# A router whose weights become the stationary operand, in four 32-column groups, with the partial sums added by a further product

## The reference

```python
def hier_moe(x, w_rg, b_rg, w_re, b_re, w_gate, w_up, w_down):
    """Top-1 expert group, then top-2 experts within it; gated-MLP experts."""
    pg = jax.nn.softmax(jnp.einsum('bld,dg->blg', x, w_rg).astype(jnp.float32) + b_rg, axis=-1)
    pg_top, g_idx = lax.top_k(pg, 1)
    le = (jnp.einsum('bld,de->ble', x, w_re).astype(jnp.float32) + b_re).reshape(B, L, N_EXPERT_GROUPS, EXPERTS_PER_GROUP)
...
    for e in range(N_EXPERTS):
        hid = jax.nn.silu(x @ w_gate[e]) * (x @ w_up[e])
        y = y + gates[..., e:e + 1] * (hid @ w_down[e])
...
x = x + mix @ w_out
x = x + hier_moe(rmsnorm(x, norm2_g), w_rg, b_rg, w_re, b_re, w_gate, w_up, w_down)
```

## Time and profile before

| | |
|---|---|
| median of three executions | 1037.68 us |
| the profiled execution | 1037.42 us, its span 1035.8 us |
| PE busy | 930.3 us, 90% of the span |
| DVE busy | 431.6 us, 42% |
| ACT busy | 161.7 us, 16% |
| POOL busy | 213.8 us, 21% |
| router, MATMUL records of full tiles | 128, 276 ns in the mean |
| expert part, first product | 593.38 us from the start |

### The profile page before, as it was taken

How to read it: one execution, slowest core, us unless ns; L and a number is a source line. 1 busy time by engine, 2 the same in 40 slices (tenths; PEclk the granted TensorE clock), 3 DMA queues, 4 the chain that set the end, 5 groups by cost and what they waited for, 6 DMA issues and landing times.

```text
span 1035.8 us, 16152 instructions
## 1 busy us (share of the span) xinstructions
PE 930.3 (90%) x6215; PEld 799.8 (77%) x6215; DVE 431.6 (42%) x1157; ACT 161.7 (16%) x454; POOL 213.8 (21%) x301
## 2 busy tenths in 40 slices
PE   6997999999999999999984099999999999999910
PEld 3953866959597786959653099999999999999910
DVE  2235363544626354552665332222222222233378
ACT  1122112121312212121220000011001011010013
POOL 1031030120303012030301322222222222222261
PEclk9999999999999999999996599999999999999965
DMA  9970706043000101010074468888888888788766
GB/s 333 291 224 20 214 1 203 2 136 98 36 27 1 62 1 41 1 41 2 1 285 66 130 217 318 314 299 325 303 300 302 316 315 313 293 295 307 255 207 231
DMA packets 91902, 184.50 MB, mean 178 GB/s; under 512 B 12933, under 2 KB 59589, under 8 KB 83666
## 3 DMA queue, kind: packets, MB, share of 16 engines
q1 hardware_dynamic: 72930, 154.86, 42.9%
q0 software_dynamic: 7328, 19.22, 5.6%
q10 hardware_dynamic: 11600, 9.84, 2.8%
HBM read 142.56 MB, written 41.31 MB: 178 GB/s over the span
## 4 chain that ended last, share of the span: by engine, by line
PE 81%; DVE 6%; DMA 2%; issue 2%; ACT 1%; ACTq 0%; POOL 0%; DVEq 0%; POOLq 0%
PE bank L1172 78%; PE bank L1177 1%; DVE win L1150 1%; DVE xbuf L1124 1%; DVE xn L1124 1%; DMA ids_d<-tokid,slots 1%; DMA win<-ids_d 0%; DMA ye_d<-wout 0%; DMA win<-ye_d,yslot 0%; PE bank L1349 0%; PE bank L1278 0%; DVE sig L783 0%; ACT nsb L641 0%; DVE hT L1124 0%; ACTq L717 0%
## 5 line engine op out<-in xcount | busy, mean ns | idle before, releaser
L1172 PE MATMUL bank<-wout,win 128*128 128x150 f32 x2048 | 265.9, 291 | 27.0 <-DVE wout L1071 27.0
L1172 PEld LDWEIGHTS bank<-wout,win 128*128 128x128 f32 x2048 | 264.2, 190 | 27.0 <-issue 27.0
L1172 PE MATMUL bank<-hT,win 128*128 128x128 f32 (+1 forms) x1536 | 180.7, 279 | 0.0
L1172 PEld LDWEIGHTS bank<-hT,win 128*128 128x128 f32 x1536 | 177.9, 192 | 0.2
L1172 PE MATMUL bank<-win 128*128 128x150 f32 x1024 | 133.6, 290 | 0.0
L1172 PE MATMUL bank<-win,hT 128*128 128x260 f32 (+3 forms) x432 | 130.9, 460 | 1.8 <-DMA win<-in_w_in 1.8
L1172 PEld LDWEIGHTS bank<-win 128*128 128x128 f32 x1024 | 132.0, 189 | 0.0
L1172 PE MATMUL bank<-wout,mixT 128*128 128x512 f32 (+1 forms) x288 | 127.0, 594 | 3.5 <-issue 2.3
L1102 DVE TENSOR_TENSOR win<-bank,win 128x150 f32<-128x150 f32 x64 | 20.2, 315 | 242.1 <-ACT win L713 242.1
L1172 PEld LDWEIGHTS bank<-win,hT 128*128 128x128 f32 (+1 forms) x432 | 78.4, 184 | 50.0 <-issue 37.5
L1172 PEld LDWEIGHTS bank<-wout,mixT 128*128 128x128 f32 (+1 forms) x288 | 50.7, 181 | 66.9 <-issue 65.1
(11 more groups left out here) (251 smaller groups left out, 776.3 us busy)
## 6 DMA issues: line engine op xcount, KB each, us to landing
win<-in_w_gate SPq DMA_DIRECT2D x32, 1024.0 KB, 5.0
win<-in_w_up SPq DMA_DIRECT2D x32, 1024.0 KB, 7.1
win<-in_w_down SPq DMA_DIRECT2D x32, 1024.0 KB, 7.1
ye_d<-zeros SPq DMA_DIRECT2D x4, 4352.0 KB, 18.0
ye_d<-wout ACTq DMA_DIRECT2D x64, 150.0 KB, 5.7
win<-in_w_in SPq DMA_DIRECT2D x4, 2048.0 KB, 19.6
xbuf<-in_x_prompt SPq DMA_DIRECT2D x8, 512.0 KB, 4.4
wout<-in_w_out SPq DMA_DIRECT2D x1, 4096.0 KB, 15.4
```

Source lines behind the costliest of these rows:

```text
L1172: return nc.tensor.matmul(out, lhsT, rhs, start=first, stop=last)
```

## The change

The operands change places. The stationary one is now a piece of `wr`, widened with zeros from 20 to 32 columns, the moving one the piece of h2T. The result comes out turned, logits on partitions and rows along the free axis. Piece k goes to partitions 32q to 32q + 31 of bank 7 with q = k mod 4, so that the bank holds four partial sums of two pieces each. DVE copies the bank out once (`partial_logits`, into lgT). A further product (`router_sums`) has lgT stationary and a 0/1 matrix `stk` (128 x 20, four identities one below the other) moving: it adds the four parts and turns them to rows at once, into columns 128 to 147 of bank 7. `logits` reads from there. `stk` and the zeros are made by POOL before the loop; `ioi` now shares the place of lgT.

```diff
-        wr = sb("wr", [P, KD, NR])
+        wr = sb("wr", [P, KD, 32])
+        stk = sb("stk", [P, NR])
+        lgT = sb("lgT", [P, P])
...
+            link(g.memset(wr[:, :, NR:32], 0.0))
+            link(g.memset(stk[:, :], 0.0))
+            for q in range(4):
+                link(g.affine_select(out=stk[:, :], in_=stk[:, :], compare_op=ALU.not_equal, fill=1.0,
+                                     base=-32 * q, pattern=[[-1, NR]], channel_multiplier=1))
...
+            def partial_logits(t):
+                R = ROWS[t]
+                after(dve, "lo_done", t + 1)
+                v.tensor_copy(lgT[:, 0:R], B[7][:, 0:R]).then_inc(S["lgT_ready"], 1)
+
             def logits(t):
                 R = ROWS[t]
-                after(dve, "lo_done", t + 1)
-                v.tensor_tensor(rt[0:R, 0:NR], B[7][0:R, 0:NR], brt[0:R, :], ALU.add).then_inc(S["lo_read"], 1)
+                after(dve, "lg_done", t + 1)
+                v.tensor_tensor(rt[0:R, 0:NR], B[7][0:R, P:P + NR], brt[0:R, :], ALU.add).then_inc(S["lo_read"], 1)
...
                 for k in range(KD):
-                    last = mm(B[7][0:R, 0:NR], h2T[:, k, 0:R], wr[:, k, :], k == 0, k == KD - 1)
+                    q = k % 4
+                    last = mm(B[7][32 * q:32 * q + 32, 0:R], wr[:, k, :], h2T[:, k, 0:R], k < 4, k >= KD - 4)
                 last.then_inc(S["lo_done"], 1)
+
+            def router_sums(t):
+
+                R = ROWS[t]
+                after(pe, "lgT_ready", t + 1)
+                mm(B[7][0:R, P:P + NR], lgT[:, 0:R], stk[:, :]).then_inc(S["lg_done"], 1)
...
+                if 2 <= i:
+                    router_sums(i - 2)
+                if DECP < i < NT:
+                    cols_by(turn_a(i), i, Q0, "q_done", range(1, 2))
...
-                    cols_by(turn_a(i), i, Q0, "q_done", range(1, 4))
+                    cols_by(turn_a(i), i, Q0, "q_done", range(2, 4))
```

More of the change, by code:

```diff
@@ L117, in hymba_step @@
         iof = sb("iof", [P, 64])
-        ioi = sb("ioi", [P, 64], I32)
+        ioi = lgT[:, 0:64].bitcast(I32)
         tokid = sb("tokid", [P, NT], I32)
@@ L208, in hymba_step @@
                  "u_ready", "dlt_ready", "pm_done", "mixb_ready", "out0_done", "out_done", "x1_ready", "rs20",
-                 "xn2_ready", "x1_stored", "h2_stored", "h2T_done", "h2T_ready", "lo_done",
+                 "xn2_ready", "x1_stored", "h2_stored", "h2T_done", "h2T_ready", "lo_done", "lgT_ready", "lg_done",
                  "lo_read", "rexp_in", "rexp", "route_ready", "rank_done", "rank_read", "slot_ready",
@@ L979, in _ @@
                     numerators(LAST)
+                    partial_logits(LAST - 1)
                     head_out(LAST)
@@ L999, in _ @@
                 if 2 <= i:
+                    partial_logits(i - 2)
                     logits(i - 2)
@@ L1386, in _ @@
                     out_of_pool(LAST, i)
+                    router_sums(LAST - 1)
                     head_transposes(LAST)
```

## The result

The changed kernel takes 1031.84 us (median of 4, 1031.37 to 1032.82) against 1038.09 for the kernel before (4, 1037.40 to 1040.21): ratio 0.9938, 95% interval 0.9920 to 0.9955. It is faster, by more than was forecast (1037.3) and past the low end of the range (1032.0).

A forecast was written before the change was run, and what follows sets the result against it. The prediction took PE to bound the kernel from 90 to 511 us. Six full tiles −1.0, tile 1 +0.27, tile 7 +0.29 and tile 8 0.0 sum to −0.4 against 1037.68, giving 1037.3 us; range 1032.0 to 1042.3.

The forecast's parts named there:

- X: PE time of a full tile's sixteen router records in four column groups; 1.21 us chosen between bounds 0.60 and 1.74.
- the lower bound of 0.60: Lower bound for the sixteen router records: all four groups overlap freely, 15 × 0.033 + 0.109 = 0.60 us.
- The other terms of a full tile: On PE beside the router records: passage 0.20 and stk product 0.22 us, against 1.79 for the old router.
- The passage into 32-column mode: On PE ahead of the router: 0.09 us, with 0.12 for the way back; 0.20 taken for the two.
- rival C: In the router every change of group costs a 0.10 us passage: about 1049 us; chance 0.07, shared with an unseen wait.
- Rival B: In the router all four groups overlap, a product's second record too: −5.2 us, 1032.5 us in all; chance 0.18.
- Tile 1: Decode rows: router records and passages stay as they are; the stk product between 128-column neighbours adds 0.27 us.
- Tile 7: Block i == NT: the copy partial_logits enters DVE's chain to head_transposes, +0.29 us; what PE saves isn't seen.
- Tile 8: Last iteration, clock 0.50: router records −1.01 us, copy, hand-over to PE and stk product +1.05; sum ±0.0.
- Hidden work: Full tiles: copy and moved work cost nothing; mix_start moves under 2 us, against 6.5 us of slack at the ranks.
- The cover of the second block of q: Its 8 products now precede the transpose of HM, moving mix_start by about 1.8 us less the router's saving; no cost.

The follow-up runs named there:

- the repetitions: The unedited changed kernel timed twice more against the kernel before: 1033.40 against 1037.29 us, ratio 0.9962, and 1032.99 against 1037.44 us, ratio 0.9965.
- the order of neighbours: The changed kernel with piece k in column group k // 2 instead of k mod 4: 1033.77 us, ratio 0.9965 to the kernel before.

## Why the prediction was wrong

**The step that failed** is the choice of X: "The two records of one product go to the same group with other weights, so the second must wait for the first, 0.109 us; only the step to the next group can overlap". Its first half is right: one group, two groups and four groups all go at 0.11 a record within a group. The second half is wrong. While one group waits for its own record, the other three go on, in both orders of the program that were run, and so the sixteen records take four rounds. X is 0.48, not 1.21, and below even the lower bound of 0.60. The bound rested on 0.033 us as "the pace at which records with 32-column weights can be issued at all". That was the pace within one group for 20 to 32 moving columns. Between groups the starts are 0.007 apart, and a row of records into one group couldn't show that.

**The other terms of a full tile.** With X = 0.48 the prediction's sum gives 0.20 + 0.48 + 0.22 − 1.79 = −0.89 a tile; the measured is −0.80. The passage into 32-column mode was as read (0.09: the last 260-column record starts at 291.57, 0.219 later the router is due at 291.79, and it starts at 291.88). Behind the router 292.45 − (291.88 + 0.48) = 0.09, and the block of q in between takes 294.34 − 292.45 = 1.89 where sixteen at 0.112 are 1.79, another 0.10. So the way back costs 0.19 and the whole passage 0.28, not 0.20, and 0.28 + 0.48 + 0.22 − 1.79 = −0.81 is the −0.80. A change of the group alone costs no such passage, as the four starts 7 ns apart show; rival C falls, and the Trainium skill (TensorEngine Tiling (Array Packing), Key Properties) is borne out: changing the mode drains the array, changing only the tile doesn't.

**Rival B**, −5.2 in all, was the case that came true, at 4 to 4.6, and had been given 0.18. Against it the prediction had written that "the two records of a product need the same columns of the array". They do, but records of other groups fill the time.

**Tile 1**, +0.27 forecast, 0.00 measured. The prediction left its router as it is because the weights have 32 columns before and after. But the change spreads its records over the groups too: x16 from 0.68 to 0.33 us, which pays for its product with stk. With one group this stage is 59.9 us, with two 59.7, with four 59.5.

```profile
173.20 0.33 PE L1187 MATMUL bank<-h2T,wr 128*32 128x32 f32 x16
```

**Tile 7**, +0.29 forecast, +0.20 measured, for the reason given, and undone by moving the copy.

**Tile 8**, ±0.0 forecast, −1.5 measured up to `logits`. The parts put into the chain were sized rightly: from the router's end at 548.99 to `logits` at 550.06 it is 1.07, against 1.05. The router's row is 1.08 long instead of 3.60; counted as the prediction does, from the starts, X at the low clock is 1.08 − 0.42 + 0.22 = 0.88, where it had 2.42 (0.42 is the length of the last record). 0.88 − 3.43 + 1.05 is the −1.5. What of it reaches the end can't be told, since the transfers behind it vary by more.

**Hidden work.** The slack named for mix_start, for POOL and for the ranks held: no wait in PE's list. The cover of the second block of q is shown by the run without it.

**The sum** of the six tiles, tile 1 and tile 7 is −4.77 + 0.0 + 0.20 = −4.6, and the means over all executions differ by 4.5 us (by 4.0 in the repetitions), so nothing of tile 8's 1.5 is seen in the total. That the first median fell 6.2 is chance from both sides: the kernel before stood at 1038.1 there, and at 1037.0 in the mean of its other 22 executions, and the changed one 1.2 to 1.6 below its repetitions. The one trace of that comparison doesn't explain the latter. In it tile 8's transposes still had the full clock, and yet with 1032.82 us it was the slowest of the four.

## What to carry to other kernels

Where a product's stationary operand needs only 32 columns, or can be turned round so that it does, its time in these runs is the number of records in a column group by what one of them costs for its moving columns (0.11 us for 128 in fp32); spread the records evenly over four groups and cost it so, plus 0.3 us for the way into the mode and back. Neither of the two orders tried was better. Do it where PE is the bound and the work behind it doesn't wait for another engine: each pause that the faster product opens can cost the clock for what follows. And of an unknown with two bounds, ask of each bound which row carries it and whether that row exercises the resource at all; the lower one here was the pace of a single group.

## What the runs showed of the hardware

Records of fp32 products with 32-column weights to different column groups start 7 ns apart (13 in the order of neighbours) and run together: sixteen of 128 moving columns take 0.48 us in four groups, 0.90 in two, 1.77 in one. A group that waits for its own record doesn't hold up the others, even with the next three records of the program for it. It holds for 128 records in a row: 14.07 us became 3.73. The way from 128-column to 32-column weights and back cost 0.28 us in all. The clock, after pauses of 1.5 and 3.6 us close together, was granted at 0.50. Behind the one wait at 90 us, which every version has, it fell in one profile (0.79 from 91 to 99 us) and stayed at 1.00 in the others, the changed kernel's three among them.
